# At most two context gathers in flight: GpSimd's next issue waits for the landing of the last but one

## The chip, the cores and the metric

One core of one Trainium2 chip. The metric is the device time of one execution of the program, in microseconds (us); lower is better. The kernel has five instruction streams: TensorE (PE, with its weight loads PEld), VectorE (DVE), ScalarE (ACT), GpSimd (POOL) and SyncE (SP), which issues most loads. 16 DMA engines move the data of both DMA queues: that of SP and that of GpSimd.

## What is computed

One layer of a hybrid network on 128 context tokens (`x_prompt`) and 512 latent tokens (`x_sample`), width 1024. A token mixer has an RWKV-7 half (scans in both directions over chunks of 64 tokens, 8 heads of 64) and a Hyena half (long convolutions); behind it stands PEER: each token picks 128 of 16384 experts, and each expert is one row `u` and one row `v` of 1024 numbers:

```python
def chunk(args):
    xc, ic, gc = args
    act = jax.nn.gelu(jnp.einsum('cd,ced->ce', xc, u_tab[ic]), approximate=False) * gc
    return jnp.einsum('ce,ced->cd', act, v_tab[ic])
```

For the 128 context tokens that is 128 dot products with gathered `u` rows and then 128 scaled additions of gathered `v` rows, with one token on each partition.

## The kernel before

The context tokens go first through both mixers and through the choice of their experts. Then, while the latent tokens' RWKV scans run, the context's PEER is done "on the side". `UNITS` has ten units (a token tile and a direction): units 0 and 1 are the context's, 2 to 9 the latents'. A unit is a chain that goes to and fro between TensorE, ScalarE and VectorE: masks (L2001 and before), six levels of a triangular solve (PE L843, L846, L878; ACT L1343, L1346), the sum blocks (PE L904 posts `r_g`, DVE L2020 waits for it; PE L920 posts `r_hm`), the outputs (PE L926 and L928, whose last matmul posts `r_yl`; DVE L2032 and ACT L1278 wait for it), and two state steps (PE L937 and L939, DVE L2037 and L2039). DVE L2044 is a unit's last VectorE instruction. Beside a unit run the preparations of the next.

A **context row** is one gather and one VectorE instruction. GpSimd issues an indirect DMA (L2318) that brings 128 rows of 4 KB, one for each token, 512 KB in all, into a slot of a ring. VectorE multiplies the slot with the tokens and sums it up (L1968, with a short read of the accumulator behind it), which posts `c_used`. VectorE's program order is written out by hand: `aside(n, l)` puts rows between the steps of a unit, 21 for each of the units 4 to 9 (17 of unit 9's stand in its solve), so rows 0 to 125 fall into these six units, `u` rows all:

```python
UNIT_ROWS = {l: 2 if l in (0, 1, 4, 7, 10) else 1 for l in range(16)}
...
if n >= 4:
    for _ in range(UNIT_ROWS.get(l, 0)):
        next(crow, None)
```

The densest stretch is eight or nine rows back to back at a unit's last levels. `C_SLOTS[n]` gives for row n the slot k, the last row that used it and the slot's use count. For rows under `WIDE_FROM` = 126 the ring has `CR + EXTRA` = 7 slots, so row n's gather waits until row n-7 is consumed (`c_used`); VectorE waits for a landing on the slot's own semaphore, `c_here[k]`, which each gather raises by 16. Rows from 126 on are issued after `gm_ok`, behind unit 9, and use another ring. SP loads tables for the stage behind unit 9 once `c_used` is 125.

Of the kernel before, what the change touches and what calls it, by code (L numbers as in the profile page):

```python
# [74 lines left out]
ROWS = (GT - 1) * 2 * SLOTS  # L75
CR, EXTRA = 4, 3
WIDE_FROM, WIDE_TO = 126, 238


def context_slots():  # L80

    slots, last, uses, out = 2 * CR, {}, {}, []
    for n in range(2 * SLOTS):
        k = n % (CR + EXTRA) if n < WIDE_FROM else (n - WIDE_FROM) % slots if n < WIDE_TO else (n - WIDE_TO) % CR
        out.append((k, last.get(k), uses.get(k, 0) + 1))
        last[k], uses[k] = n, uses.get(k, 0) + 1
    return out, [uses[k] for k in range(CR, slots)]


C_SLOTS, C_USES = context_slots()  # L90
# [39 lines left out]
def program(nc, a, outs):  # L130
# [7 lines left out]
    with ExitStack() as ctx:  # L138
        def sem(name):
            return ctx.enter_context(nc.semaphore(name))  # L140
# [209 lines left out]
        def S(name):  # L350
            if name not in s:
                s[name] = sem(name)
            return s[name]
# [8 lines left out]
        c_here = [sem(f"c_here{i}") for i in range(CR)] + row_here[0:CR]  # L362
# [1936 lines left out]
        @block.gpsimd  # L2299
        def _(pool):  # L2300
            pool.wait_ge(S("ada_mm"), 12)
            pool.memset(sn, 0.0).then_inc(S("sn_zero"), 1)
            pool.wait_ge(S("in_mm"), NIN)
            for v in (gblk, hc, st2[0]):
                pool.memset(v, 0.0).then_inc(S("sn_zero"), 1)

            pool.wait_ge(S("eid_ok"), 1)
            pool.wait_ge(S("out_state"), 16 * 16)
            pool.wait_ge(S("sn_ok"), 1)
            pool.wait_ge(S("gm_ok"), 1)  # L2310
            for n in range(2 * SLOTS):
                e, m = divmod(n, SLOTS)
                k, prev, use = C_SLOTS[n]
                if prev is not None:
                    pool.wait_ge(S("c_used"), prev + 1)
                if n == WIDE_FROM:
                    pool.wait_ge(S("gm_ok"), NT)
                pool.indirect_dma_start((gring_u if n < WIDE_FROM else gring_c)[k], None, a[("peer_u", "peer_v")[e]][0],  # L2318
                                        bass.IndirectOffsetOnAxis(ap=ids_c[:, m:m + 1], axis=0)).then_inc(c_here[k], 16)

            pool.wait_ge(S("h2T_ok"), KD)
            pool.tensor_copy(hTd, hTl[:, :, LL - ND:LL]).then_inc(S("hTd_ok"), 1)
            pool.wait_ge(S("x_out"), 32)
            for n in range(ROWS):
                t, e, m = n // (2 * SLOTS), n // SLOTS % 2, n % SLOTS
                if e == 0 and m == 0:
                    pool.wait_ge(S("eid_ok"), t + 2)
                if n >= RING:
                    pool.wait_ge(S("g_used"), n - RING + 1)
                pool.indirect_dma_start(gring[:, n % RING, :], None, a[("peer_u", "peer_v")[e]][0],  # L2330
                                        bass.IndirectOffsetOnAxis(ap=ids[:, t, m:m + 1], axis=0)).then_inc(row_here[n % RING], 16)
# [83 lines left out]
```

## Time and profile before

| | us |
|---|---|
| median of 3 runs | 2557.89 (2556.46 to 2564.34) |
| the profiled execution, its own time | 2563.7 |
| its span | 2561.8 |
| stage of the change (first context gather to the end of unit 9) | 614 to 953 of the span |

The span is divided by what each engine does at each moment. An engine's row in a timeline gives its start and its duration; the bracket behind it gives the idle time just before it and what ended that. "remote" there stands for a release that the profile can't put down to an instruction's end. The stage of the change is 13% of the span.

### The profile page before, as it was taken

The numbers are of one execution on the slowest core, as the hardware profiler recorded it, in microseconds if no ns is written. First come the engines' busy times: TensorE is split into PE (matmuls) and PEld (weight loads), VectorE is DVE, ScalarE is ACT, GpSimd is POOL, SyncE is SP. The second block draws the span as 40 slices with busy tenths as digits, with TensorE's granted clock in tenths as the row PEclk, the third lists the DMA queues.
The fourth block names the chain that finished last, engine by engine and source line by source line (L and its number), as shares of the span: only waits on it lengthen the run. The fifth ranks groups of instructions, "written<-read, shape, count | busy, mean of one in ns | idle before, by whom it ended". The sixth has DMA issues, their size and how long they took to land.

```text
span 2561.8 us, 42536 instructions
## 1 busy us (share of the span) xinstructions
PE 2308.0 (90%) x17474; PEld 1607.0 (63%) x17474; DVE 1777.8 (69%) x3489; ACT 469.8 (18%) x994; POOL 957.1 (37%) x777
## 2 busy tenths in 40 slices
PE   6999978788888879998799699999999999999997
PEld 3555547567667654344588677776776677775664
DVE  2111364266888766776898967899999888875777
ACT  2111233243343311001222101000001000000101
POOL 0000000001555532444520016767665667764652
PEclk9999989888999979998899599999999999999998
DMA  8341120501666743777871048999999999999997
GB/s 332 136 163 47 66 83 20 188 2 59 212 223 208 234 169 128 287 248 280 320 291 68 2 156 329 398 372 402 408 405 343 409 401 400 389 398 411 409 409 295
DMA packets 163931, 646.94 MB, mean 253 GB/s; under 512 B 21062, under 2 KB 21958, under 8 KB 158298
## 3 DMA queue, kind: packets, MB, share of 16 engines
q0 software_dynamic: 110592, 402.70, 41.9%
q1 hardware_dynamic: 53146, 241.52, 24.4%
q8 instruction: 139, 2.28, 0.4%
q14 instruction: 54, 0.44, 0.1%
HBM read 635.50 MB, written 8.65 MB: 251 GB/s over the span
## 4 chain that ended last, share of the span: by engine, by line
PE 65%; DVE 13%; DMA 10%; issue 6%; ACT 4%; another core or an unknown queue 1%; POOL 1%; SPq 0%; DVEq 0%; POOLq 0%; ACTq 0%
PE ps L1118 11%; PE ps L1129 11%; DMA arena<-in_peer_v,arena 8%; PE ps L613 7%; PE ps L1140 6%; PE ps L1094 4%; PE ps L1034 2%; PE ps L1001 2%; PE ps L1059 2%; PE ps L1044 2%; PE ps L617 2%; DVE arena L1968 1%; DVE arena L2150 1%; PE ps L806 1%
## 5 line engine op out<-in xcount | busy, mean ns | idle before, releaser
L1129 PE MATMUL ps<-arena 128*128 128x512 f32 x1024 | 470.3, 603 | 25.4 <-DVE arena L2189 24.0
L1118 PE MATMUL ps<-arena 128*128 128x256 f32 x2048 | 478.8, 387 | 1.8 <-issue 1.8
L2330 POOL DMA_INDIRECT arena<-in_peer_u,arena x256 | 343.3, 1341 | 349.7 <-DVE arena L1935 192.2
L1118 PEld LDWEIGHTS ps<-arena 128*128 128x128 f32 x2048 | 390.2, 194 | 71.0 <-issue 22.3
L2330 POOL DMA_INDIRECT arena<-in_peer_v,arena x256 | 295.0, 1152 | 211.0 <-DVE arena L2150 144.9
L2318 POOL DMA_INDIRECT arena<-in_peer_u,arena x128 | 168.8, 1319 | 543.7 <-DVE arena L1935 324.4
L2150 DVE SCALAR_TENSOR_TENSOR arena<-arena 128x1024 f32<-128x1024 f32 x252 | 314.7, 1283 | 73.1 <-DMA arena<-in_peer_v,arena 71.0
L1129 PEld LDWEIGHTS ps<-arena 128*128 128x128 f32 x1024 | 196.1, 193 | 228.2 <-issue 219.5
L2145 DVE SCALAR_TENSOR_TENSOR arena<-arena 128x1024 bf16<-128x1024 f32 x256 | 302.1, 1221 | 30.7 <-DMA arena<-in_peer_u,arena 27.6
L1140 PEld LDWEIGHTS ps<-arena 128*128 128x128 bf16 x3072 | 206.0, 156 | 69.6 <-issue 46.7
L1140 PE MATMUL ps<-arena 128*128 128x32 bf16 x3072 | 208.8, 243 | 23.4 <-DVE arena L2182 22.5
L2318 POOL DMA_INDIRECT arena<-in_peer_v,arena x128 | 144.3, 1127 | 182.3 <-DVE arena L1972 149.6
L1569 DVE SCALAR_TENSOR_TENSOR arena<-ps,arena 128x504 f32<-128x504 f32 x48 | 35.7, 743 | 201.0 <-ACT arena L1216 200.2
L613 PE MATMUL ps<-arena 128*128 128x512 f32 x384 | 170.0, 596 | 0.7 <-ACT arena L1188 0.7
L1972 DVE SCALAR_TENSOR_TENSOR arena<-arena 128x1024 f32<-128x1024 f32 x126 | 156.0, 1283 | 11.5 <-DMA arena<-in_peer_v,arena 11.4
L1968 DVE SCALAR_TENSOR_TENSOR arena<-arena 128x1024 bf16<-128x1024 f32 x128 | 151.7, 1221 | 7.8 <-DMA arena<-in_peer_u,arena 6.3
L1454 ACT ACTIVATE arena<-ps 128x256 f32<-128x256 f32 x128 | 48.9, 383 | 516.0 <-PE ps L1118 456.2
L1462 ACT ACTIVATE arena<-ps 128x256 f32<-128x256 f32 x128 | 49.1, 384 | 502.9 <-PE ps L1140 435.4
L2177 DVE TENSOR_TENSOR arena<-arena 128x1024 bf16<-128x1024 bf16 x128 | 88.2, 689 | 67.7 <-PE ps L1140 55.5
L613 PEld LDWEIGHTS ps<-arena 128*128 128x128 f32 x384 | 71.1, 190 | 85.4 <-issue 85.4
L1094 PE MATMUL ps<-arena 128*128 128x256 f32 x512 | 117.7, 384 | 0.9 <-issue 0.9
L1094 PEld LDWEIGHTS ps<-arena 128*128 128x128 f32 x512 | 96.4, 193 | 13.3 <-issue 1.1
(365 smaller groups left out, 3138.3 us busy)
## 6 DMA issues: line engine op xcount, KB each, us to landing
arena<-in_uT SPq DMA_DIRECT2D x128, 512.0 KB
arena<-in_peer_v SPq DMA_DIRECT2D x128, 512.0 KB
arena<-in_w_ada SPq DMA_DIRECT2D x12, 2048.0 KB, 21.5
arena<-in_peer_wq SPq DMA_DIRECT2D x12, 2048.0 KB, 9.2
arena<-in_w_in SPq DMA_DIRECT2D x6, 2048.0 KB, 8.6
arena<-in_w_out SPq DMA_DIRECT2D x4, 2048.0 KB, 10.7
arena<-in_peer_u,arena POOLq DMA_INDIRECT x384
arena<-in_peer_v,arena POOLq DMA_INDIRECT x384
```

What stands on the lines that cost most here:

```text
L613: pe.matmul(ps[:, n % 2, :], w[:, k, P * f:P * f + P], hT[:, k, LC:T], start=(k == 0), stop=(k == KD - 1))
L1094: m = pe.matmul(ps[:, n % 2, 0:ND], ring[slot_of["wq", j]][:, k, P * f:P * f + P], half[:, k, :], start=(k == 0), stop=(k == KD - 1))
L1118: m = pe.matmul(ps[:, 4 + i % 2, 0:ND], us[i % UB][:, k, :], hTd[:, k, :], start=(k == 0), stop=(k == KD - 1))
L1129: m = pe.matmul(ps[:, 2 * r + c, :], sgel[:, i % SBUFS, P * r:P * r + P], vs[i % VB][:, 512 * c:512 * c + 512], start=(i == 0), stop=(i == ...
L1140: m = pe.matmul(ps[:, 6 + g % 2, QI * c:QI * c + QI], one_j[:, g % 2, :, c], one_i[g % 2][:, k, :, c], start=(k == 0), stop=(k == 2))
L1968: m = V.scalar_tensor_tensor(junk_c[c % 2], slot, 1.0, h2_c, ALU.mult, ALU.mult, accum_out=dots_c[:, m:m + 1])
L1972: m = V.scalar_tensor_tensor(dst, slot, coef_c[:, m:m + 1], dst, ALU.mult, ALU.add)
L2145: V.scalar_tensor_tensor(junk[:, m % 2, :], slot, 1.0, h2[:, 1 + t, :], ALU.mult, ALU.mult, accum_out=dots[:, m:m + 1]).then_inc(S("g_used ...
L2150: V.scalar_tensor_tensor(acc[:, m % 2, :], slot, coef[:, m:m + 1], acc[:, m % 2, :], ALU.mult, ALU.add).then_inc(S("g_used"), 1)
L2177: V.tensor_tensor(one_j[:, g % 2, :, :], iota8[:, 0, :, :], col(1, P), ALU.is_equal)
L2318: pool.indirect_dma_start((gring_u if n < WIDE_FROM else gring_c)[k], None, a[("peer_u", "peer_v")[e]][0], bass.IndirectOffsetOnAxis(ap=id ...
L2330: pool.indirect_dma_start(gring[:, n % RING, :], None, a[("peer_u", "peer_v")[e]][0], bass.IndirectOffsetOnAxis(ap=ids[:, t, m:m + 1], axi ...
```

## The change

For rows 2 to 125, GpSimd waits, besides the wait for the slot, until the gather of row n-2 has landed. Rows from 126 on, and the 512 gathers of the latent tokens, are issued as before.

```diff
+FLIGHT = 2
...
                 if prev is not None:
                     pool.wait_ge(S("c_used"), prev + 1)
+                if FLIGHT <= n < WIDE_FROM:
+                    k_ago, _, use_ago = C_SLOTS[n - FLIGHT]
+                    pool.wait_ge(c_here[k_ago], 16 * use_ago)
                 if n == WIDE_FROM:
                     pool.wait_ge(S("gm_ok"), NT)
```

## Rows read from the trace of the kernel before

**Rows 1.** GpSimd's instructions from 640 to 935 us, grouped: busy, mean ns, idle before.

```profile
L2318 POOL DMA_INDIRECT arena<-in_peer_u,arena x119 | 159.9, 1343 | 149.4 <-DVE arena L1968 123.2 <-issue 26.2
```

**Rows 2.** VectorE's last instruction of units 3, 8 and 9: start, duration, instruction.

```profile
641.80 0.68 DVE L2044 TENSOR_TENSOR arena<-ps,arena 128x512 f32<-128x512 f32 x1
...
900.29 0.68 DVE L2044 TENSOR_TENSOR arena<-ps,arena 128x512 f32<-128x512 f32 x1
...
951.95 0.68 DVE L2044 TENSOR_TENSOR arena<-ps,arena 128x512 f32<-128x512 f32 x1
```

**Rows 3.** Busy time in unit 5: PE, PEld, DVE, ACT, POOL; clock, DMA share, GB/s.

```profile
691.00:742.00 51.00, 41.25 (x829) 34.73 (x827) 42.10 (x78) 19.33 (x38) 27.72 (x21) 0.97 0.68 219
```

**Rows 4.** VectorE's waits from 640 to 952 us: in total, times, longest.

```profile
DVE arena L2032 <- remote: 21.8, 4, 5.4
...
DVE arena L1968 <- DMA arena<-in_peer_u,arena: 6.3, 5, 4.2
```

**Rows 5.** VectorE's timeline: end of unit 5, and the same instruction in unit 9.

```profile
729.26 1.22 DVE L1968 SCALAR_TENSOR_TENSOR arena<-arena 128x1024 bf16<-128x1024 f32 x1
...
735.92 0.69 DVE L2032 TENSOR_TENSOR arena<-ps,arena 128x512 f32<-128x512 f32 x1 [5.44 <-remote]
...
944.77 0.69 DVE L2032 TENSOR_TENSOR arena<-ps,arena 128x512 f32<-128x512 f32 x1
```

**Rows 6.** TensorE's timeline: the last matmuls of L928 in units 5 and 9.

```profile
731.38 0.34 PE L928 MATMUL ps<-arena 64*64 64x64 f32 x4
...
944.44 0.28 PE L928 MATMUL ps<-arena 64*64 64x64 f32 x4
```

**Rows 7.** GpSimd's timeline: its issues around that wait of unit 5.

```profile
731.59 0.94 POOL L2318 DMA_INDIRECT arena<-in_peer_u,arena  x1 [0.30 <-issue]
...
734.09 0.94 POOL L2318 DMA_INDIRECT arena<-in_peer_u,arena  x1 [0.30 <-issue]
```

**Rows 8.** ScalarE's timeline in unit 3, at GpSimd's first seven issues.

```profile
619.21 0.38 ACT L1343 ACTIVATE arena<-ps 128x256 f32<-128x256 f32 x1 [2.98 <-remote]
...
624.29 0.39 ACT L1346 ACTIVATE arena<-ps 128x256 f32<-128x256 f32 x1 [2.33 <-PE ps L878]
```

**Rows 9.** GpSimd's timeline: issues of rows 7, 17, 48, 112, 113 and 121.

```profile
647.38 1.68 POOL L2318 DMA_INDIRECT arena<-in_peer_u,arena  x1 [24.54 <-DVE arena L1968]
...
669.27 1.99 POOL L2318 DMA_INDIRECT arena<-in_peer_u,arena  x1 [0.30 <-issue]
...
742.09 0.94 POOL L2318 DMA_INDIRECT arena<-in_peer_u,arena  x1 [3.13 <-DVE arena L1968]
...
905.97 7.41 POOL L2318 DMA_INDIRECT arena<-in_peer_u,arena  x1 [7.14 <-DVE arena L1968]
913.69 0.95 POOL L2318 DMA_INDIRECT arena<-in_peer_u,arena  x1 [0.30 <-issue]
...
924.93 0.98 POOL L2318 DMA_INDIRECT arena<-in_peer_u,arena  x1 [0.30 <-issue]
```

**Rows 10.** VectorE's timeline: end of row 41; rows 111 to 113, 121; unit 9's L2020.

```profile
741.74 0.08 DVE L1968 DVE_READ_ACCUMULATOR arena<-arena 128x1 f32 x1
...
911.35 1.21 DVE L1968 SCALAR_TENSOR_TENSOR arena<-arena 128x1024 bf16<-128x1024 f32 x1
...
916.80 1.23 DVE L1968 SCALAR_TENSOR_TENSOR arena<-arena 128x1024 bf16<-128x1024 f32 x1 [4.23 <-DMA arena<-in_peer_u,arena]
...
918.82 1.22 DVE L1968 SCALAR_TENSOR_TENSOR arena<-arena 128x1024 bf16<-128x1024 f32 x1 [0.78 <-DMA arena<-in_peer_u,arena]
...
931.35 1.23 DVE L1968 SCALAR_TENSOR_TENSOR arena<-arena 128x1024 bf16<-128x1024 f32 x1
940.04 1.53 DVE L2020 TENSOR_TENSOR arena<-ps,arena 64x256 f32<-64x256 f32 x4 [7.47 <-PE ps L904]
```

**Rows 11.** DMA from 741 to 749 us: GB/s in 40 equal slices of 0.2 us.

```profile
GB/s 471 389 307 123 20 0 0 0 0 0 0 0 82 102 143 61 82 102 369 389 369 410 328 225 21 20 0 0 0 0 0 0 0 0 0 0 0 0 0 0
```

## The prediction

> **What bounds the kernel now.** I began with GpSimd's instructions, grouped, over the stage. The line that changes has 119 issues from 640 to 935 us with 159.9 us of GpSimd's time, and GpSimd idles before them for 149.4 us, 123.2 of these until VectorE has freed a slot [rows 1]: the engine itself is no bound, so the question is only when rows are there, and what the gathers do to others meanwhile. The stage is units 4 to 9, rows 0 to 125. By VectorE's last instruction of each unit, the five units 4 to 8 last from 641.80 to 900.29 us, 258.5 us or 51.7 each, and unit 9 another 51.7 [rows 2].
>
> The busy table of unit 5 says who is nearest to full: VectorE 42.1 of 51 us, TensorE 41.3, GpSimd 27.7, and DMA at 0.68 of its time [rows 3]. So VectorE, with 21 rows in every unit, is the nearest bound. The list of its waits shows what fills the rest: four waits of L2032, 21.8 us, the longest of 5.4, that end on "remote"; and only 6.3 us on gathers [rows 4]. Rows are today nearly always there in time.
>
> The "remote" waits are the interesting ones. L2032 waits for `r_yl`, posted by the last matmul of L928. In unit 5 those matmuls end at 731.72, and VectorE, idle since row 39's end at 730.48, starts at 735.92 [rows 5, 6]: 4.2 us from matmul to wake-up. In unit 9 the same pair stands at 944.72 and 944.77, 0.05 us apart. The difference between them is in GpSimd's timeline: in unit 5 it issues three gathers 1.25 us apart from 731.59 on, the last from 734.09 to 735.03, and the release comes 0.9 us behind that [rows 7]; in unit 9 the last gather was issued long before. ScalarE shows the like in unit 3, when the first seven gathers are issued in one go: 2.98 us "remote" and 2.33 us on L878 [rows 8]. I read this as: **posts of TensorE come late while three or more gathers are under way**. That is what the change could give back.
>
> **What the change adds.** Nothing is removed. 124 waits are added on GpSimd's queue. Behind a waiting issue stand only further gathers; who waits for those is VectorE's L1968, in order in front of the units' own steps. A wait that is already satisfied costs nearly nothing. What matters is the pace: with two in flight, two gathers take the time from one issue to its landing as GpSimd sees it. Its terms:
> - the issue itself: 1.34 us mean of 119 [rows 1]; bounds 0.94 and 1.99 [rows 9].
> - from the issue's end to the landing. Row 112 is issued until 913.38 and VectorE, which waits for it, starts at 916.80: 3.42 us, alone. Row 113 with others behind it: 914.64 to 918.82, 4.18 us [rows 9, 10]. Row 48, alone, has its issue's end at 743.03 and its last slice of traffic at 746.2: 3.2 us [rows 9, 11]. Bounds 3.2 and 4.18; with always one other gather on the way I take the middle of 3.42 and 4.0, 3.7.
> - GpSimd's wake-up: VectorE ends row 41 at 741.82, GpSimd starts the issue that waited for it at 742.09: 0.27 us [rows 9, 10].
>
> Sum: 1.34 + 3.7 + 0.27 = 5.3 us for two gathers, **2.65 us for each**. Bounds: (0.94 + 3.2 + 0.27) / 2 = 2.2, and (1.99 + 4.18 + 0.27) / 2 = 3.2.
>
> Demand: without the late posts a unit could last 51 - 5.4 = 45 us, 2.15 us for each of 21 rows; even today's 51.7 asks for one in 2.46. Supply at 2.65 is slower than either, so **the gathers become the bound of the stage** and the ring of seven drains: GpSimd's 123.2 us of waiting for slots [rows 1] go, and the late posts of TensorE, whether they vanish or not, are hidden behind it.
>
> **The sum**, from issue to issue. Today row 7 is issued at 647.38 and row 121, the last of unit 9's solve, at 924.93: 114 gathers in 277.6 us, 2.43 each [rows 9].
> - 114 x 2.65 = 302.1 us: +24.5.
> - Behind it: today 27.7 us pass from 924.93 to the end of unit 9 at 952.63 [rows 2], because L2020 waits 7.47 us for TensorE, itself held up by late posts [rows 10]. After: issue 1.3, landing 3.7, row 1.15, then L2020 to the end as today (952.63 - 940.04 = 12.6), and about 1 us as row 124 comes late between them: 19.8. That is -7.9.
> - Unit 3: the late posts at the first seven gathers shrink, as from the third on they go out one by one; 2.98 + 2.33 = 5.3 us of ScalarE's waits on the solve's chain [rows 8], taken as 5.5 with TensorE's own idle time behind them: -5.5.
> - Behind unit 9 nothing is changed: rows from 126 on, and SP's tables, start from unit 9's end.
>
> 24.5 - 7.9 - 5.5 = **+11 us**: 2575 for the profiled execution's own 2563.7, which lies 5.8 above the median; so I forecast 2569 against the median 2557.9. The break-even pace is 2.65 - 11.1 / 114 = 2.55; each 0.1 us of pace is 11.4 us of time, which is why the range is wide.
>
> **What the Trainium skill says of two of these terms.** A row issued just after a landing starts together with VectorE's own row, and issues that meet VectorE's rows are the long ones: 1.99 us at row 17, 7.41 us at row 112, whose issue ends at 913.38, 0.8 us after row 111, the last of seven rows back to back [rows 9, 10]. The Trainium skill, "SBUF — State Buffer", section "Who interferes with whom", says that a VectorE instruction in certain modes, or with two SBUF inputs against GpSimd reads, takes a shared port for its whole length and the other engine blocks; the rows agree, and it speaks against this change. With every issue at 1.99 the pace would be (1.99 + 3.7 + 0.27) / 2 = 2.98, and the sum +49.
> The Trainium skill, "DMA: Bandwidth & Descriptors", section "Anatomy of one DMA — SWDGE (gpsimd) path", gives 2.0 us plus the bytes over 436 GB/s for one such DMA, an estimate of 3.2 us for 512 KB. By that two gathers take 3.5 us and the pace is 1.7, faster than any demand here; row 48 took 0.94 + 3.2 = 4.1 from its issue's start, so the trace is above it.
>
> **Rivals.**
> - *Supply keeps up and the late posts go* (ends faster). At the lower bound of 2.2 us a gather a unit of 45.1 us gets 20.5 of its 21 rows, so VectorE is the bound. Gain: 21.8 us of L2032 [rows 4] and about 5 for unit 6, where the wait lies elsewhere; 5.5 in unit 3; some 3 in unit 9: -35, 2523. It decides below 2.3 us a gather. For it: lone gathers are at 3.2 us. Against it: only 0.94 us issues give it, and the mean is 1.34.
> - *Supply binds, but at 2.5 or less*: -6 to -25. Nothing but the size of one term separates it from the forecast.
> - *Supply binds and the port makes it worse*: most issues at 1.99 or longer, +30 to +50.
> - *The change does little*: the waits are mostly satisfied, as in the dense stretch today's issues are already 2.29 us apart (1.99 + 0.30) [rows 9]. Then 2558. Against it: row 18's issue at 2.29 us behind row 17's would have to wait for row 16, whose landing takes 1.34 + 3.7 from its start.
>
> **Chances.** Supply binds near 2.65 (forecast, slower): 0.46; it binds between 2.48 and 2.62, within 0.3% (7.7 us, about what a measurement of this kernel tells from no change): 0.17; it binds faster than that: 0.10; supply keeps up: 0.15; port worse: 0.06; little changes: 0.06. So faster 0.25, same 0.23, slower 0.52. Range: pace 2.45 gives -12, 2.85 gives +34; the case of -35 and the port case pull on both sides: 2540 to 2598.
>
> **What would show it.** Right: GpSimd's waits end on DMA, not on VectorE; issues lie some 2.65 us apart through units 4 to 9; L1968 waits on DMA grow from 6.3 us to tens; L2032's "remote" waits are gone or short; units 4 to 8 last some 55 us; unit 3 ends some 5 us earlier. Wrong if units 4 to 8 come to 45 us with few waits on DMA (the landing is nearer to 3.2 and issues short), or if "remote" waits go on with two in flight, which would make my reading of them wrong though not the sum.

## The result, and the profile of the changed kernel

The kernel before takes 2557.18 us (median of 4 runs, 2556.36 to 2564.34), the changed one 2599.91 (4 runs, 2596.23 to 2604.78): a ratio of 1.0165, 95% interval 1.0136 to 1.0194. It is 43 us slower; I had forecast 11. The profiled execution took 2596.8 us, its span is 2595.0, 33.2 over that of before.

GpSimd's gathers from 640 us to behind the last issue of unit 9's solve, grouped; it answers to [rows 1]:

```profile
L2322 POOL DMA_INDIRECT arena<-in_peer_u,arena x119 | 149.7, 1258 | 199.3 <-DMA arena<-in_peer_u,arena 162.0 <-DVE arena L1969 28.2 <-issue 9.1
```

VectorE's last instruction of units 3, 8 and 9 (all of VectorE's lines up to here are one higher), for [rows 2]:

```profile
641.31 0.68 DVE L2045 TENSOR_TENSOR arena<-ps,arena 128x512 f32<-128x512 f32 x1
...
930.96 0.69 DVE L2045 TENSOR_TENSOR arena<-ps,arena 128x512 f32<-128x512 f32 x1
...
992.47 0.68 DVE L2045 TENSOR_TENSOR arena<-ps,arena 128x512 f32<-128x512 f32 x1
```

The busy table of unit 5, with columns as in [rows 3]:

```profile
695.00:755.00 60.00, 42.99 (x824) 36.07 (x824) 42.67 (x78) 19.11 (x38) 25.17 (x22) 0.83 0.62 184
```

VectorE's waits from 640 to 993 us, for [rows 4]:

```profile
DVE arena L1969 <- DMA arena<-in_peer_u,arena: 90.1, 66, 4.1
DVE arena L1724 <- ACT arena L1262: 4.9, 2, 3.1
DVE arena L2038 <- PE ps L940: 4.7, 2, 4.1
```

What ends GpSimd's idle time is now DMA, 162.0 us, and VectorE's waits on gathers went from 6.3 us to 90.1. "remote" is gone from VectorE's list. Units 4 to 8 last 57.9 us each, (930.96 - 641.31) / 5, against 51.7, with much the same work in a unit, 41 to 43 us on TensorE and 42 to 43 on VectorE: only waiting was added, and the DMA share fell from 0.68 to 0.62. The gathers bound the stage, as forecast.

The end of unit 5, VectorE's timeline, where [rows 5] showed 5.44 us on "remote":

```profile
745.16 1.23 DVE L1969 SCALAR_TENSOR_TENSOR arena<-arena 128x1024 bf16<-128x1024 f32 x1 [0.45 <-DMA arena<-in_peer_u,arena]
746.31 0.08 DVE L1969 DVE_READ_ACCUMULATOR arena<-arena 128x1 f32 x1
746.31 0.69 DVE L2033 TENSOR_TENSOR arena<-ps,arena 128x512 f32<-128x512 f32 x1
748.04 1.23 DVE L1969 SCALAR_TENSOR_TENSOR arena<-arena 128x1024 bf16<-128x1024 f32 x1 [1.04 <-DMA arena<-in_peer_u,arena]
```

L2033 follows its row at once; it is the rows that wait. GpSimd's timeline from the issue of row 7 to that of row 121, with the stretch of unit 9 in which landings come one after the other, for [rows 9]:

```profile
646.88 1.68 POOL L2322 DMA_INDIRECT arena<-in_peer_u,arena  x1 [12.16 <-DVE arena L1969]
...
655.29 1.32 POOL L2322 DMA_INDIRECT arena<-in_peer_u,arena  x1 [4.44 <-DVE arena L1969]
...
955.47 1.30 POOL L2322 DMA_INDIRECT arena<-in_peer_u,arena  x1 [2.76 <-DMA arena<-in_peer_u,arena]
957.89 1.30 POOL L2322 DMA_INDIRECT arena<-in_peer_u,arena  x1 [1.12 <-DMA arena<-in_peer_u,arena]
960.80 1.30 POOL L2322 DMA_INDIRECT arena<-in_peer_u,arena  x1 [1.61 <-DMA arena<-in_peer_u,arena]
...
971.69 1.30 POOL L2322 DMA_INDIRECT arena<-in_peer_u,arena  x1 [1.81 <-DMA arena<-in_peer_u,arena]
```

VectorE's rows that the same landings release, for [rows 10]:

```profile
957.15 1.22 DVE L1969 SCALAR_TENSOR_TENSOR arena<-arena 128x1024 bf16<-128x1024 f32 x1 [1.19 <-DMA arena<-in_peer_u,arena]
...
960.06 1.23 DVE L1969 SCALAR_TENSOR_TENSOR arena<-arena 128x1024 bf16<-128x1024 f32 x1 [1.67 <-DMA arena<-in_peer_u,arena]
...
962.30 1.23 DVE L1969 SCALAR_TENSOR_TENSOR arena<-arena 128x1024 bf16<-128x1024 f32 x1 [1.01 <-DMA arena<-in_peer_u,arena]
```

Follow one gather. It is issued at 955.47 and lands for VectorE at 960.06: 4.59 us. That landing also releases the next but one issue, at 960.80, 0.74 us after VectorE. (Below, this time from the start of VectorE's row to the start of the issue released by the same landing is called the wake-up.) The issue at 957.89 lands at 962.30, 4.41 us. The cycle for two gathers is 960.80 - 955.47 = 5.33 us here, and over the six from 955.47 to 971.69 the pace is 16.22 / 6 = 2.70 us. Over all 114, from 646.88 to 971.69, it is 324.8 / 114 = **2.85 us**, against 2.43 before.

ScalarE in unit 3 at the first gathers, for [rows 8]:

```profile
621.63 0.39 ACT L1344 ACTIVATE arena<-ps 128x256 f32<-128x256 f32 x1 [1.32 <-PE ps L844]
...
623.73 0.39 ACT L1347 ACTIVATE arena<-ps 128x256 f32<-128x256 f32 x1 [0.47 <-PE ps L879]
```

The 2.98 us and 2.33 us have become 1.32 and 0.47. DMA from 955 to 963 us in 40 slices of 0.2 us, for [rows 11]; between gathers the engines stand still, once for four slices:

```profile
GB/s 369 287 246 143 225 123 102 41 20 0 0 0 164 143 123 102 164 369 369 430 410 266 82 0 164 102 123 102 225 389 410 430 369 307 0 0 0 0 20 184
```

**The difference, added up.** At unit 3's start the changed kernel is 4.1 us late, before a gather is issued (592.56 against 588.48). Unit 3 gives back 4.6. 114 gathers cost 47.3 more. From row 121's issue to unit 9's end 21.5 us pass instead of 27.7: -6.2. So unit 9 ends 40.5 us later, at 993.15. The latter stages gave back 7 in this execution; the change does not touch them.

### The profile page after: what moved, and what is told of

It is laid out like the page before. It is cut to its first block, busy times and chain, and to the rows that moved or that the text cites. A ratio compares the mean times of both kernels' runs of the same rounds, so it can differ in the third digit from the quotient of the medians.

```text
span 2595.0 us, 42655 instructions
## 1 busy us (share of the span) xinstructions
PE 2292.5 (88%) x17474; PEld 1597.9 (62%) x17474; DVE 1782.1 (69%) x3489; ACT 469.9 (18%) x994; POOL 942.8 (36%) x777
## 4 chain that ended last, share of the span: by engine, by line
PE 57%; DMA 19%; DVE 12%; issue 6%; ACT 2%; POOL 1%; another core or an unknown queue 1%; SPq 0%; DVEq 0%; POOLq 0%; ACTq 0%
DMA arena<-in_peer_u,arena 10%; PE ps L1119 10%; PE ps L1130 9%; DMA arena<-in_peer_v,arena 8%; PE ps L614 6%; PE ps L1141 5%; PE ps L1095 4%; DVE arena L2151 2%; PE ps L1045 2%; PE ps L1002 2%; PE ps L1035 2%; PE ps L1060 2%; PE ps L618 2%; PE ps L807 1%
## 5 line engine op out<-in xcount | busy, mean ns | idle before, releaser
L2334 POOL DMA_INDIRECT arena<-in_peer_u,arena x256 | 338.1, 1321 | 348.0 <-DVE arena L1936 190.3
L2322 POOL DMA_INDIRECT arena<-in_peer_u,arena x128 | 158.6, 1239 | 597.2 <-DVE arena L1936 328.2
L1969 DVE SCALAR_TENSOR_TENSOR arena<-arena 128x1024 bf16<-128x1024 f32 x128 | 155.0, 1223 | 90.7 <-DMA arena<-in_peer_u,arena 90.1
```

Of the source, the lines that this page charges most:

```text
L1969: m = V.scalar_tensor_tensor(junk_c[c % 2], slot, 1.0, h2_c, ALU.mult, ALU.mult, accum_out=dots_c[:, m:m + 1])
```

## The experiments

Four chips were used, called P, Q, R and S here; P in two jobs, the others in one each. They are part of the result: the kernel before takes 2559 to 2561 us on P, 2558 on Q, but 2504 on R and 2506 on S. The chip of the first pair, above, is not on record; its kernel before takes 2557. Ratios are to the kernel before on the same chip in the same job. A pace is that of one traced execution, from row 7's issue to row 121's; the changed kernel has 2.85 and, traced again (e13), 2.84. A "limit" is the number of gathers under way, `FLIGHT`.

| kernel | chip | median us | ratio, 95% |
|---|---|---|---|
| e1, landing's wait in front of the slot's | P | 2593.5 | 1.0131 [1.0108, 1.0154] |
| e2, VectorE's rows of 32 columns | P | 2576.3, one run | (1.006) |
| e3, both | P | 2573.8, one run | (1.005) |
| e11, limit of one | R | 2898.0, one run | (1.158) |
| e9, 2 KB gathers, limit of two | R | 2543.3 | 1.0152 [1.0116, 1.0188] |
| e15, the same | P | 2549.4 | 0.9970 [0.9948, 0.9993] |
| e10, 2 KB gathers, no effective limit | R | 2505.4 | 0.9999 [0.9983, 1.0016] |
| e14, the same | P | 2565.7 | 1.0021 [0.9991, 1.0052] |
| e12, kernel before | P | 2560.6 | 0.9995 [0.9963, 1.0026] |
| e13, changed kernel | P | 2594.1 | 1.0137 [1.0094, 1.0180] |
| e5, limit of two for rows 2 to 6 only | Q | 2556.7 | 0.9982 [0.9956, 1.0009] |
| e7, wait that is always satisfied | Q | 2564.8 | 1.0019 [0.9991, 1.0046] |
| e6, limit of four | Q | 2544.5 | 0.9933 [0.9908, 0.9958] |
| e4, limit of three | P | 2535.1 | 0.9906 [0.9877, 0.9935] |
| e18, the same | S | 2511.8 | 1.0042 [1.0024, 1.0061] |
| e8, limit of three, waits in e1's order | Q | 2533.1 | 0.9867 [0.9821, 0.9913] |
| e16, 0.96 us memset between issues | S | 2538.3 | 1.0149 [1.0113, 1.0184] |
| e17, 0.54 us memset between issues | S | 2514.4 | 1.0032 [1.0015, 1.0050] |

### What makes the pace 2.85 us

**e1** swaps the two waits, with nothing else changed:

```diff
+                if FLIGHT <= n < WIDE_FROM:
+                    ...
+                    pool.wait_ge(c_here[k_ago], 16 * use_ago)
                 if prev is not None:
                     pool.wait_ge(S("c_used"), prev + 1)
-                if FLIGHT <= n < WIDE_FROM:
-                    ...
```

> The changed kernel with its two waits in the other order: first the landing of row n-2, then the slot. In the changed kernel's trace the landing wait is an instruction of its own; it passes at 957.35 us, together with VectorE's row, and the gather behind it starts only at 958.09, 0.74 us later, while a gather that carries its wait itself starts 0.27 us after its release. Theory W (the separate wait's 0.74 us is what was missing in the forecast pace of 2.65 us a gather, measured 2.85): if the swap puts the landing wait onto the gather, the pace falls by half of 0.47 us, to 2.62, and the time by some 25 us. Theory P (an issue that meets a VectorE row ends 0.8 us after that row whatever it started at): issues start earlier but last 1.8 us instead of 1.3, the pace stays at 2.85 and the time within 6 us of the changed kernel.

Its timeline in unit 9, GpSimd and then VectorE:

```profile
955.40 1.80 POOL L2322 DMA_INDIRECT arena<-in_peer_u,arena  x1 [0.82 <-DMA arena<-in_peer_u,arena]
958.38 1.80 POOL L2322 DMA_INDIRECT arena<-in_peer_u,arena  x1 [1.17 <-DMA arena<-in_peer_u,arena]
```

```profile
955.17 1.23 DVE L1969 SCALAR_TENSOR_TENSOR arena<-arena 128x1024 bf16<-128x1024 f32 x1 [1.38 <-DMA arena<-in_peer_u,arena]
...
958.14 1.22 DVE L1969 SCALAR_TENSOR_TENSOR arena<-arena 128x1024 bf16<-128x1024 f32 x1 [1.74 <-DMA arena<-in_peer_u,arena]
```

The issue now starts 0.23 us behind VectorE's row instead of 0.74, my 0.27. But it lasts 1.80 us instead of 1.30. Both kernels' issues end 0.8 us after the row does: 958.38 + 1.80 = 960.18 against 958.14 + 1.22 = 959.36 here, 957.89 + 1.30 = 959.19 against 957.15 + 1.22 = 958.37 in the changed kernel. So 0.5 us of a late wake-up is hidden under an issue that can't end before VectorE's row anyway, and taking it away brings little: the mean issue is 1.54 us against 1.26, the pace is 2.75, and the ratio 1.0131 beside the changed kernel's 1.0137 on the same chip (e13), which is no difference that shows. (The trace is of the fastest of e1's four executions, 2581.8 us, so even the 2.75 may flatter it.)

**e2** takes the row away as an obstacle: VectorE works on 32 of the 1024 columns of rows 0 to 125, so the sums are not those of the reference. **e3** does that and swaps the waits.

```diff
-m = V.scalar_tensor_tensor(junk_c[c % 2], slot, 1.0, h2_c, ...)
+w = 32 if c < WIDE_FROM else D
+m = V.scalar_tensor_tensor(junk_c[c % 2][:, 0:w], slot[:, 0:w], 1.0, h2_c[:, 0:w], ...)
```

> The changed kernel, but VectorE multiplies and sums only the first 32 of 1024 columns of rows 0 to 125, so its row instruction shrinks from 1.22 us to about 0.1 (the context output is wrong by that part). The gathers and waits are the same. Theory P (rows of VectorE hold up the issues): issues fall from 1.26 to 0.94 us, and as they start at 1.08 us after the last packet, the pace falls from 2.85 to about (1.08 + 0.94 + 3.0) / 2 = 2.5 us. Theory D (the landing itself takes 4 us with another gather on the way): pace stays at 2.75 or more.

> Both edits: narrow VectorE rows and the landing wait before the slot wait. Without VectorE rows in the way an earlier start must show: if the swap moves the landing wait onto the gather, the pace is (0.6 + 0.94 + 3.0) / 2 = 2.3 us against 2.5 with the narrow rows alone. If it is the same as that one, the 0.74 us of start-up belong to any wait for a landing, or the order in the program doesn't decide which wait the gather carries.

GpSimd's gathers from 600 to 985 us, of e2 and of e3:

```profile
L2323 POOL DMA_INDIRECT arena<-in_peer_u,arena x126 | 120.3, 955 | 553.7 <-DVE arena L1936 325.0 <-DVE arena L1970 189.7 <-DMA arena<-in_peer_u,arena 34.5
```

```profile
L2323 POOL DMA_INDIRECT arena<-in_peer_u,arena x126 | 123.4, 980 | 541.8 <-DVE arena L1936 323.6 <-DVE arena L1970 161.5 <-DMA arena<-in_peer_u,arena 53.3
```

(The short row ends with the landing that released it, which is why the idle time is put down to VectorE.) The mean issue falls from 1.26 to 0.96 us, so meeting VectorE's rows did cost 0.3 us of each. The pace falls to 2.72 only, and to 2.64 with the swap: not meeting a row is worth 0.13 us, and together with the wake-up 0.2. Both forecasts, 2.5 and 2.3, were too low. In part that is because the gathers answer: over the rows that waited for one, the time from the issue's end to the row is 3.7 us in the mean in the changed kernel and in e2, but 4.1 in e3, whose issues follow the landings soonest. The short rows also leave VectorE more time, so the demand is not quite the same; and each is one execution, against two changed kernels' traces that differ by 0.01. What is left, 2 x 2.64 = 5.3 us for two, is issue and landing.

**e11** sets `FLIGHT = 1`.

> Limit of one: each issue waits for the landing of the gather in front of it, so the pace is the whole cycle of a lone gather. By the changed kernel's terms: issue 1.26 (0.94 alone, 1.30 when it meets VectorE's row, and every one starts together with a row here), landing 3.1, and 1.1 from the last packet to the next issue: 5.4 to 5.5 us each. From row 7 to row 121 that is 114 x 5.45 = 621 us in place of 325, so some 300 us over the changed kernel, 2890. Theory serial transfers: in the changed kernel a gather also waits for the one in front of it on the DMA engines, so a lone one lands sooner, in 2.9 or less from the issue's end, and the pace is under 5.3. Rival: landing is as long alone, 3.25, and half of the cycle, 2.85, is just the limit of two: pace 5.7.

Its pace is 5.43 us: the cycle of one lone gather. GpSimd, then VectorE's row released by the first of the two:

```profile
1255.20 1.30 POOL L2322 DMA_INDIRECT arena<-in_peer_u,arena  x1 [3.88 <-DMA arena<-in_peer_u,arena]
1260.75 1.30 POOL L2322 DMA_INDIRECT arena<-in_peer_u,arena  x1 [4.24 <-DMA arena<-in_peer_u,arena]
```

```profile
1260.01 1.23 DVE L1969 SCALAR_TENSOR_TENSOR arena<-arena 128x1024 bf16<-128x1024 f32 x1 [4.31 <-DMA arena<-in_peer_u,arena]
```

4.8 us from issue to row and 0.74 to the next issue. Half of 5.43 is 2.72, against 2.85 with the limit of two: a second gather lengthens the cycle by 0.3 us. By the mean over the rows that waited for a gather, all of it is between issue's end and row, 3.4 us alone and 3.7 with a second. (e11 ran on R and the changed kernel did not, but the 2 KB gathers with the limit of two, below, have nearly the same pace on R and on P.) So the theory of serial transfers, which asked for 2.9 us or less alone and a pace under 5.3, falls: what sets the pace here is the latency of one cycle, divided by the limit. **e9** and **e15** halve the bytes (2 KB a token, from a view of the table with rows of 512; VectorE's row is as long as before and reads stale numbers in its second half):

```diff
+if n < WIDE_FROM:
+    dst_g, src_g = dst_g[:, 0:512], src_g.rearrange("r (b c) -> (r b) c", c=512)
```

> The changed kernel, but each gather of rows 0 to 125 brings 128 rows of 2 KB (from a view of the table with rows of 512 numbers) in place of 4 KB; VectorE's row is as long as before and reads stale data in its second half, so the numbers that come out are not the reference's. In the changed kernel two gathers took 1.26 + 3.25 + 1.36 = 5.9 us less the overlap, 2.85 each. Theory transfer: of the 3.25 us from the issue's end to the last packet some 2.3 are the transfer, which runs one gather after another; halved, the pace falls by about 0.5 to 0.6, to 2.3, VectorE's waits on gathers fall from 90 us to under 30, and the time is some 60 us under the changed kernel, ratio to before 0.985 to 0.995. Rival fixed cost: the landing is start-up and completion, the bytes matter little: pace 2.75 or more, ratio over 1.01.

> 2 KB gathers with the limit of two. The trace of the last such run has a pace of 2.44 us against 2.85 with 4 KB: the landing was 2.2 us behind the issue's end in place of 3.25. Theory transfer: 40 to 45 us below the changed kernel on the same chip, whichever chip it is. Rival: part of that difference was the chip's, and it is 25 us or less.

The pace is 2.44 on R and 2.41 on P. In e15, GpSimd and then VectorE:

```profile
906.33 1.31 POOL L2325 DMA_INDIRECT arena<-in_peer_u,arena  x1 [1.99 <-DMA arena<-in_peer_u,arena]
```

```profile
910.03 1.23 DVE L1969 SCALAR_TENSOR_TENSOR arena<-arena 128x1024 bf16<-128x1024 f32 x1 [1.78 <-DMA arena<-in_peer_u,arena]
```

3.70 us from issue to row instead of 4.4 to 4.6. That is one gather; in the mean over the rows that waited, the time from the issue's end to the row is 2.7 us against 3.6 in e13 on the same chip, so 256 KB are worth 0.9 us, and on P the time is 2549.4 against 2594.1 of e13: 45 us. The forecast of 40 to 45 was right, and a part that depends on bytes and a larger one that does not both stand. e9 missed both of its forecasts of the ratio: it is 1.0152 although the pace fell, as the kernel before is 55 us faster on R. The Trainium skill, "DMA: Bandwidth & Descriptors", section "Anatomy of one DMA — SWDGE (gpsimd) path", has such a split, and its 436 GB/s give an estimate of 0.6 us for 256 KB; the runs show 0.9.

### What makes TensorE's posts late, and where

**e5** applies the limit to rows 2 to 6 alone (`if FLIGHT <= n < CR + EXTRA`).

> Limit of two for rows 2 to 6 only, the burst of unit 3; from row 7 on the kernel before. Theory late posts: unit 3's chain is shortened by the 5 us that ScalarE waited there, unit 3 lasts 48.7 us as in the changed kernel instead of 53.3, and nothing of it is lost later: ratio 0.998, some 5 us faster. Rival: the 4.6 us seen in unit 3 of the changed kernel are given back in unit 4, whose ring is not yet full: no change. If unit 3 lasts 53 us, the shortening there came from something other than the first seven gathers.

Unit 3 lasts 49.1 us, 587.79 to 636.87, against 53.3. The ratio of 0.9982 is 4.6 us, near the 5.5 of my step, but the interval reaches to 1.0009 and the medians stand 1.5 us apart: the shortening of the unit is shown, its worth for the whole is not. (The unit's 49.1 us are from the fastest of twelve executions, but every trace with a limit of two has 48.7 to 49.4 us there, and the kernel before (twice), the limit of four, e7 and e14 have 53.0 to 56.1.)

**e7** sets `FLIGHT = 7`, so that the waits are there but always satisfied.

> The added wait looks seven gathers back, which the slot's wait already implies, so it never holds anything up: the price of the added wait instructions alone. Theory: the wait is its own instruction on GpSimd and lies between the slot's release and the issue, some 0.05 to 0.1 us for each of the issues that waited for a slot, which VectorE doesn't feel as the ring is full: within 0.2% of the kernel before. Rival: each added wait costs GpSimd 0.5 us or more when it stands in front of an issue (in the changed kernel an issue starts 0.74 us behind the wait's end); then issues in a burst lie 2 us apart instead of 1.25, fewer gathers overlap, and late posts shrink by that: 10 us or more faster, units 4 to 8 under 50 us.

1.0019, within the noise: the added instructions cost nothing to be seen, and they don't thin out the late posts (19.3 us of VectorE's waits on "remote").

**e10** and **e14** are the 2 KB gathers with `FLIGHT = 7`.

> The same 2 KB gathers for rows 0 to 125 without any effective limit (the added wait looks seven rows back and is always satisfied). Tells what makes posts of TensorE late. Theory backlog: late posts come when packets of gathers queue up behind each other; with half the bytes the queue drains in about 1.3 us a gather, as fast as GpSimd issues, the waits of VectorE on remote in units 4 to 9 fall from 21.8 us to under 5, and the time is 25 to 35 us under before, ratio 0.987 to 0.990. Rival issue: it is the issuing by GpSimd itself, or the count of gathers under way, whatever their size: remote waits of 10 us or more stay, and the ratio is 0.995 to 1.002.

This run gave the surprise. On R its list of waits has no "remote" of VectorE, its units 4 to 8 last 44.6 us, and yet it is no faster than the kernel before there, which is itself 55 us faster than on P. So two readings were left, the size of the gathers or the chip, and the four kernels e12 to e15 were run together to tell them apart.

> 2 KB gathers for rows 0 to 125, no effective limit (stale second halves, so other numbers come out). Theory chip: late posts depend on the chip only, so where before takes 2558 this has waits on remote of some 20 us too and the ratio is 1.0 on every chip. Theory backlog: late posts come with queued packets, so on a chip where before takes 2558 the waits vanish, units 4 to 8 last 44.5 us and the ratio is 0.982 to 0.987; on a chip of 2503 us nothing is left to gain and the ratio is 1.0.

> The kernel before, for its trace on the same chip as the three kernels beside it. Ratio 1.0. Theory chip: where before takes some 2503 us its units 4 to 8 last 44 to 46 us each and no wait of VectorE on remote is over 1 us; where it takes some 2558 they last 51 to 52 and the waits are some 20 us. Rival: the units last 51 us on a 2503 us chip too, and the 54 us lie elsewhere (in the latent experts' gathers behind the stage).

> The changed kernel on the same chip. The pace of a gather under the limit is DMA and GpSimd, 2.8 to 2.9 us on any chip, units 4 to 8 57 to 58 us. So the ratio depends on before: 1.016 where before takes 2558, 1.035 to 1.04 where it takes 2503. Rival: what makes the chip faster also shortens the landing, and the ratio is 1.016 there too.

They fell on P. VectorE's waits from 600 to 960 us in e14:

```profile
DVE arena L2021 <- PE ps L905: 23.2, 3, 16.9
DVE arena L2033 <- remote: 21.9, 4, 5.5
```

The same kernel that had none on R has 21.9 us of late posts on P, as many as the kernel before with 4 KB [rows 4], and takes 2565.7 us instead of 2505.4. e10 and e14 are one program, so it is not the gathers' bytes: late posts go with the **chip**, as far as P in two jobs and the others in one each can tell; what differs between the chips is not known. e12, the kernel before on P, has 22.1 us of them and units 4 to 8 of 53.0 us. On P the changed kernel is 1.0137 [1.0094, 1.0180], with a pace of 2.84. No trace of the kernel before on R or S was taken, so that its own units last 44.6 us there is inferred, from e10 having its time.

Counted from the traces' semaphore events between 600 and 950 us, posts of TensorE that came over 1.5 us behind their matmul (from there on the profile puts a wait down to "remote"; those over 10 us left out), by the issues that GpSimd had begun in the 4 us before:

```
                                  0 or 1     2          3 or more
before                            1 of 106   6 of 72    15 of 24
e12 (before, P)                   1 of 111   8 of 68    9 of 24
e14 (2 KB, no limit, P)           1 of 104   7 of 75    16 of 26
e4 (limit of three, P)            1 of 62    6 of 136   0 of 14
changed kernel                    0 of 132   0 of 64    -
e10 (2 KB, no limit, R)           0 of 74    0 of 114   0 of 29
```

A post has to be paired with its matmul by time, and some are missing from the traces; a stricter pairing gives 12 of 19, 8 of 21 and 12 of 22 in the last column's first three lines, and leaves the rest as it is but for a few. By gathers under way at that moment (from the issue to the last part of the landing), e14 has 12 late ones of 87 with two under way and e4 none of 99 with three. So my words "while three or more gathers are under way" are wrong as a rule: a count of gathers does not predict it; a dense row of issues goes with it better, on the chips that have late posts at all. **e16** and **e17** were to test that: a memset of the slot and a wait for it hold GpSimd up between issues, with no wait for a landing.

```diff
+if 2 <= n < WIDE_FROM:
+    pool.memset(gring_u[k][:, 0:1024], 0.0).then_inc(...)      # 512 in e17
+    pool.wait_ge(...)
```

> The kernel before, with no limit on gathers under way, but a memset of the slot (128x1024, 0.95 us on GpSimd) and a wait for it between the slot's wait and the issue of rows 2 to 125: issues can't follow each other closer than some 2.5 us (issue 1.0 to 1.3, memset 0.95, waits 0.3 to 0.6) in place of 1.25. Theory spacing: late posts come where three or more issues fall into a few us, so on a chip where before takes 2558 us the waits of VectorE on remote go from 21.8 us to under 5; the pace, 2.4 to 2.6, then binds, and the time is within 0.5% of before. If the memset waits for VectorE's rows the pace is nearer to 2.8 and the ratio 1.01. Rival under way: what counts is gathers under way; at 2.5 us apart that is two, so the waits go too; this run alone doesn't tell them apart, the 2 KB gathers do.

> The same with a memset of 128x512, some 0.5 us: issues at least 2.0 to 2.1 us apart. The supply is then above VectorE's demand of 2.1 to 2.2 us a row, and 2 or 3 gathers are under way in bursts. Theory spacing: waits on remote under 5 us on a chip of 2558, units 4 to 8 at 45 to 47 us, ratio 0.984 to 0.992, as with the limit of three or better. Rival under way: with three under way late posts stay, 10 us or more of remote waits, ratio 0.994 to 1.0.

They fell on S, where there is probably nothing to give back (no "remote" wait in either, nor in e18 on S), so the cause stays open: spacing, or something in the way of posts and descriptors that this chip does not have. They show only what spacing costs: paces of 2.37 and 2.19 us, and 33 and 9 us of time.

### Which limit

**e4**, **e6** and **e8**: `FLIGHT` is 3, 4, and 3 with e1's order of the waits.

> The changed kernel with three gathers in flight instead of two (FLIGHT = 3). Theory of the pace (in-flight gathers divided by one gather's round trip of 5.7 us): 1.9 us a gather, faster than the 2.15 that VectorE asks for, so VectorE is the bound of units 4 to 8 again. Theory H (TensorE's posts come late from three in flight on): the late posts are back in part, units 4 to 8 at 48 to 51 us, time 2535 to 2560. Rival (posts are late only with four in flight or with issues 1.25 us apart): units of 45 us, time about 2520.

> Limit of four. The trace of the kernel before has the long late posts of TensorE (over 2 us) with three and four gathers under way. Theory late posts: four give them back in part, so it lies between the limit of three (0.991) and no limit (1.0), units 4 to 8 at 47 to 51 us. Rival pace: what the limit of three still lacks is supply (VectorE waited 13.9 us on gathers there), so four is faster than three, 0.985 or lower, with VectorE's waits on gathers under 10 us.

> Limit of three, with the wait for the landing placed in front of the wait for the slot. With the limit of two that order took 0.1 us off the pace and 6 us of time. Theory: with three, GpSimd's waits on landings are 50.9 us only and VectorE's on gathers 13.9 us, so the same order takes off 0 to 3 us: 0.989 to 0.991. Rival: the instruction order changes which late posts occur, and time moves by 5 us or more either way.

VectorE's waits in e4 from 600 to 960 us:

```profile
DVE arena L1969 <- DMA arena<-in_peer_u,arena: 13.9, 12, 4.5
DVE arena L2021 <- PE ps L905: 11.2, 1, 11.2
DVE arena L1724 <- ACT arena L1262: 9.5, 5, 3.4
```

With three, a gather comes every 2.24 us (1.9 was expected), units 4 to 8 last (873.86 - 642.44) / 5 = 46.3 us, and it is **faster than both kernels**: 0.9906. Late posts are not all gone: ScalarE still has 8.8 us of waits on "remote", VectorE 0.7. Nor is the cycle what it was with one or two: an issue that a landing released starts 6.7 us behind the issue of that gather in the mean, against 5.7 with two and 5.4 with one. Four gives less, 0.9933, 13.7 us by the medians for 25.9 with three; VectorE has one "remote" wait of 4.1 us of L2033 again. The swapped order has the lowest ratio, 0.9867, but its interval overlaps e4's, and each median is 25 to 26 us below its chip's kernel before.

**e18** is e4 again on S.

> The limit of three again, on the chip of the two kernels beside it. Where before takes 2558 us: 0.9906 as the first time, within its interval of 0.9877 to 0.9935. Where before takes 2503: there are no late posts to give back and the pace of 2.24 us is above VectorE's demand of 2.13 by 0.1: 5 to 15 us slower, ratio 1.002 to 1.006.

1.0042 [1.0024, 1.0061]: where posts are not late, the limit of three costs 6 us, as forecast, at a pace of 2.18. What the limit is worth depends on the chip, with opposite signs.

## Why the prediction was wrong in size, step by step

- **The bound after the change.** Right. GpSimd waits on DMA, VectorE on gathers, 6.3 to 90.1 us, and GpSimd's waits on slots fall from 123.2 to 28.2.
- **The pace of 2.65 us.** This is the step that failed: it is 2.85, and 0.20 x 114 = 22.8 us are nearly all of the difference between forecast and profile (+47.3 for +24.5). Of its three terms, two held and GpSimd's wake-up was mis-sized:
  - the issue, 1.34 forecast, is 1.26;
  - issue's end to VectorE's row, 3.7 forecast, is 3.7 in the mean over the 63 rows from 7 to 121 that waited for a gather, with half of them under 3.5 and single ones up to 5.3. The steady stretch shown above is at the short end (959.19 + 3.11 = 962.30; 956.77 + 3.29 = 960.06), and with it a cycle of 1.30 + 3.3 + 0.74 = 5.3, near my 5.3 and not that of the whole stage;
  - GpSimd's wake-up, **0.27 forecast, is 0.74** behind VectorE's, and 0.78 in the mean. I had taken it from an issue that waited for a slot alone, with no row of VectorE's in its way. Here the landing is the second of two waits, and in the trace the second stands as an instruction of its own in front of the issue, which carries only the first.

  With these the cycle is 1.26 + 3.68 + 0.78 = 5.72 and the pace 2.86. The half microsecond more of wake-up is 0.25 us of pace, 29 us in all, of which the shorter issue gives back 5. The forecast also took wake-up and issue as independent, and they are not: the landing that releases the issue starts VectorE's row too. e1 shows that the 0.27 is there to be had, and that the issue then lasts 0.5 us longer. So the true term is the end of the issue: from the row's start it is 1.22 + 0.8 = 2.0 us, whichever way the waits stand, where the forecast had 0.27 + 1.34 = 1.6.
- **The end of the stage**, -7.9: it is -6.2. 27.7 became 21.5, and L2021 no longer waits 7.47 us there.
- **Unit 3**, -5.5: it is -4.6 (48.75 against 53.32 us), and e5, with the limit on the first seven alone, has -4.2 of it.
- **Late posts.** That they cost, and go with the limit, was right: no "remote" in the changed kernel. That the number under way causes them was wrong, and that they are on only some chips could not be seen in one trace. What does cause them stays open.
- **The rule on VectorE's port.** The Trainium skill, "SBUF — State Buffer", section "Who interferes with whom", says that a VectorE instruction with two inputs in SBUF contends with a GpSimd instruction that reads SBUF, over a shared port. The runs agree: 1.26 us of mean issue with rows of 1024 columns, 0.96 with rows of 32 (the row has two such inputs, and the issue reads its row numbers from SBUF; that it is the port, no run here shows). It is worth 0.13 us of pace by e2, some 15 us, not the +49 of all issues at 1.99, since the late wake-up had the issue begin halfway into the row.
- **The rivals.** "Supply keeps up and the late posts go" was wrong for two but is nearly what e4 does with three, at a pace of 2.24, as its point of decision of 2.3 said. Its -35 was -24 to -26. "The port makes it worse", +30 to +50, gave the size that was measured and half of the mechanism: the mean issue is 1.26 us, not 1.99, but VectorE's row does set where it ends. The measured time, 2600, also lies 2 us above the whole range.

## What to carry to other kernels

Under a limit on transfers under way each transfer takes the latency of one full cycle divided by the limit: measure that cycle from the issue to the row that starts with the landing, add the wake-up and what the next issue meets, and compare it with the demand of the densest stretch, not of the mean. The cycle itself grows with the limit (5.4, 5.7 and 6.7 us here with one, two and three), so it can't be divided by a limit at which it was not measured. Then take the next limit up: with two the supply was 2.85 against a demand of some 2.1 to 2.2 us, with three 2.24, and on a chip with late posts the sign changed. And before a stall is called the kernel's, look at the same kernel on a second chip.

## What the runs showed of the hardware

- The same kernel takes 2558 to 2561 us on two chips and 2504 to 2506 on two others. The one kernel traced on both kinds (e10 and e14) has no "remote" wait of VectorE on one and 21.9 us on the other, and units 4 to 8 of 44.6 and 51.8 us each.
- An issue by GpSimd that begins within one of VectorE's rows ends 0.8 us after the row, whether it began 0.04, 0.23 or 0.74 us into it (77 of the changed kernel's 126 issues, 75 of e1's). One that begins 0.8 us before a row ends 0.3 us before the row does, and lasts 1.68 us instead of 0.94.
- Of two waits in front of an issue the one written first rides on the issue itself; the one written last is an instruction of its own in front of it. When that one was the landing's, the issue started 0.74 us after VectorE had started on the same landing; when the landing's rode on the issue (e1), 0.23 us after it.
- TensorE's granted clock was 0.83 in unit 5 of the changed kernel, against 0.97 before [rows 3]; TensorE was busy for 43.0 of 60 us there, against 41.3 of 51. VectorE's waits in that stage are on gathers (90.1 us), not on TensorE (4.7), so the clock did not set its length.
